# Giving the two chunk halves of a blockwise triangular inverse one signal each and grouping TensorE's matmuls by half

## What is computed

```python
def step(state, inp):
    r_t, w_t, k_t, v_t, a_t, b_t = inp
    sa = jnp.einsum('bhij,bhj->bhi', state, a_t)
    state = (state * w_t[:, :, None, :] + sa[..., None] * b_t[:, :, None, :]
             + v_t[..., None] * k_t[:, :, None, :])
    return state, jnp.einsum('bhij,bhj->bhi', state, r_t)
```

## Time and profile before

| | us |
|---|---|
| median of 3 runs (2155.95 to 2160.34) | 2159.74 |
| the profiled execution | 2153.14 |
| its span | 2151.0 |
| TensorE busy, share of the span | 1959.3, 91% |
| VectorE busy | 988.5, 46% |
| ScalarE busy | 792.0, 37% |

### The profile page before, as it was taken

How to read it: one execution, slowest core, us unless ns; L and a number is a source line. 1 busy time by engine, 2 the same in 40 slices (tenths; PEclk the granted TensorE clock), 3 DMA queues, 4 the chain that set the end, 5 groups by cost and what they waited for, 6 DMA issues and landing times.

```text
span 2151.0 us, 35394 instructions
## 1 busy us (share of the span) xinstructions
PE 1959.3 (91%) x15150; PEld 1549.5 (72%) x15150; DVE 988.5 (46%) x1642; ACT 792.0 (37%) x1323; POOL 142.8 (7%) x126
## 2 busy tenths in 40 slices
PE   3988677777788999999999999999999989999999
PEld 2777365555566788888877777777777777888887
DVE  7443345455544444443335445445445444444422
ACT  4333333333432322222244445445445533222211
POOL 0000323333321000000000000000000000000000
PEclk9999678898998999999999999999999999999999
DMA  2222600000011333333332122222122112333332
GB/s 97 79 78 89 204 2 8 7 8 7 5 64 50 88 96 95 95 101 94 98 89 79 59 69 69 60 69 69 59 69 69 40 59 83 95 96 98 101 97 97
DMA packets 57395, 155.49 MB, mean 72 GB/s; under 512 B 5575, under 2 KB 22135, under 8 KB 57240
## 3 DMA queue, kind: packets, MB, share of 16 engines
q1 hardware_dynamic: 57144, 153.15, 23.5%
q10 hardware_dynamic: 96, 0.07, 0.0%
HBM read 151.03 MB, written 11.61 MB: 76 GB/s over the span
## 4 chain that ended last, share of the span: by engine, by line
PE 86%; DVE 8%; issue 3%; ACT 2%; DMA 1%; POOL 0%; SPq 0%; DVEq 0%; ACTq 0%; POOLq 0%
PE bank L437 83%; PE bank L440 3%; DVE r L1323 1%; DVE f L1409 1%; DVE f L1417 1%; DVE f L1335 1%; DVE f L1392 1%; ACT f L1234 1%; DVE f L1371 0%; DVE f L1422 0%; DVE f L1451 0%; DMA f<-xT 0%; DVE f L1378 0%; DVE f L1465 0%; DVE f L1470 0%
## 5 line engine op out<-in xcount | busy, mean ns | idle before, releaser
L437 PE MATMUL bank<-r 128*128 128x512 f32 x5952 | 1399.9, 396 | 39.5 <-DVE r L1323 22.7
L437 PEld LDWEIGHTS bank<-r 128*128 128x128 f32 x5952 | 1125.2, 190 | 294.1 <-issue 34.6
L437 PE MATMUL bank<-f 64*64 64x64 f32 (+6 forms) x8734 | 525.6, 261 | 143.1 <-DVE f L1302 23.6
L437 PEld LDWEIGHTS bank<-f 64*64 64x64 f32 (+3 forms) x8734 | 375.9, 151 | 281.0 <-issue 147.1
L1291 DVE TENSOR_TENSOR r<-f,r 128x1024 fp32r<-128x1024 f32 x248 | 303.8, 1225 | 502.9 <-ACT r L957 502.6
L957 ACT ACTIVATE r<-f 128x1024 fp32r<-128x1024 f32 x248 | 260.0, 1049 | 157.8 <-PE bank L437 138.2
L1615 DVE TENSOR_TENSOR f<-bank,f 128x512 f32<-128x512 f32 x72 | 55.5, 771 | 134.6 <-PE bank L437 134.3
L1182 ACT ACTIVATE r<-f 128x512 fp32r<-128x512 f32 x44 | 27.8, 632 | 221.9 <-DVE f L1584 221.9
L1208 ACT ACTIVATE f<-bank,f 128x512 f32<-128x512 f32 x48 | 33.0, 687 | 173.5 <-PE bank L437 173.5
L440 PE MATMUL bank<-f 128*128 128x128 f32 x464 | 73.8, 284 | 5.9 <-ACT f L1234 5.5
L1409 DVE TENSOR_TENSOR f<-bank,f 64x512 f32<-64x512 f32 x80 | 55.0, 688 | 50.5 <-PE bank L437 49.2
(11 more groups left out here) (99 smaller groups left out, 965.5 us busy)
## 6 DMA issues: line engine op xcount, KB each, us to landing
f<-stream SPq DMA_DIRECT2D x248, 512.0 KB, 3.6
bias_copies<-bias_rows SPq DMA_DIRECT2D x3, 3072.0 KB, 24.4
f<-xT SPq DMA_DIRECT2D x16, 256.0 KB, 4.3
f<-lora_out SPq DMA_DIRECT2D x16, 128.0 KB, 2.4
f<-bias_copies SPq DMA_DIRECT2D x16, 128.0 KB, 3.3
f<-bias_copies SPq DMA_DIRECT2D x32, 64.0 KB, 3.0
outT<-f SPq DMA_DIRECT2D x8, 256.0 KB, 4.6
f<-const SPq DMA_DIRECT2D x1, 576.0 KB, 4.0
```

Source lines behind the costliest of these rows:

```text
L437: return nc.tensor.matmul(out, lhsT, rhs, start=start, stop=stop, skip_group_check=True)
```

## The change

The two signals `x_ps` and `x_sb`, and `u_ps`, become one signal for each half. `off_diagonal` and `next_inverse` issue all matmuls of half 0 first, then all of half 1, with a wait for each half's own input ahead of its block. VectorE masks half 0 when half 0's products are there and then waits for half 1's. ScalarE's copy waits for half 0 alone, VectorE's for half 1 alone. The matmuls, masks and copies themselves stay the same.

```diff
@@ TensorE, off_diagonal and next_inverse
-                else:
-                    pe.wait_ge(s["u0_sb"], (N_LEV - 1) * hp + n - 1)
-                    pe.wait_ge(s["u1_sb"], (N_LEV - 1) * hp + n - 1)
-                for q in range(NT):
-                    for h in range(2):
-                        for e in range(2):
+                for e in range(2):
+                    if n > 1:
+                        pe.wait_ge(s[f"u{e}_sb"], (N_LEV - 1) * hp + n - 1)
+                    for q in range(NT):
+                        for h in range(2):
                             last = mm(banks[2 + e][CH * e:CH * (e + 1), (h * 4 + q) * CH:(h * 4 + q + 1) * CH],
                                       half(score(O_BU, hp, h, q, 0), 1 - e), half(block64(tu(hp, e), h, q), 1 - e))
-                last.then_inc(s["x_ps"], 1)
+                    last.then_inc(s[f"x_ps{e}"], 1)
...
-                pe.wait_ge(s["x_sb"], 2 * ((N_LEV - 1) * hp + n))
...
-                        if n < N_LEV - 1:
-                            for e in range(2):
-                                mm(to(e, 1 - e), u(e), x(e))
-                        for e in range(2):
-                            last = mm(to(e, e), x(e), u(e))
-                last.then_inc(s["u_ps"], 1)
+                for e in range(2):
+                    pe.wait_ge(s[f"x_sb{e}"], (N_LEV - 1) * hp + n)
+                    for q in range(NT):
+                        for h in range(2):
+                            u, x = half(block64(tu(hp, e), h, q), e), half(block64(O_XI, h, q), e)
+                            to = lambda side: banks[4 + e][CH * side:CH * (side + 1), (h * 4 + q) * CH:(h * 4 + q + 1) * CH]
+                            if n < N_LEV - 1:
+                                mm(to(1 - e), u, x)
+                            last = mm(to(e), x, u)
+                    last.then_inc(s[f"u_ps{e}"], 1)
@@ ScalarE, keep_inverse
-                act.wait_ge(s["u_ps"], (N_LEV - 1) * hp + n)
+                act.wait_ge(s["u_ps0"], (N_LEV - 1) * hp + n)
@@ VectorE, x_masked and keep_inverse
-                dve.wait_ge(s["x_ps"], (N_LEV - 1) * hp + n)
                 for e in range(2):
+                    dve.wait_ge(s[f"x_ps{e}"], (N_LEV - 1) * hp + n)
...
-                       bc(lev, (0, 8), (1, CH)), ALU.mult).then_inc(s["x_sb"], 1)
+                       bc(lev, (0, 8), (1, CH)), ALU.mult).then_inc(s[f"x_sb{e}"], 1)
...
-                dve.wait_ge(s["u_ps"], (N_LEV - 1) * hp + n)
+                dve.wait_ge(s["u_ps1"], (N_LEV - 1) * hp + n)
```

## The result

| | before | changed |
|---|---|---|
| median us | 2160.04 (4 runs, 2155.95 to 2161.38) | 2246.87 (4 runs, 2218.28 to 2279.57) |
| ratio | | 1.0352, 95% interval 1.0271 to 1.0433 |
| profiled execution, its span | 2153.14, 2151.0 | 2218.28, 2216.2 |

What follows compares the result with a forecast made beforehand. The inverses' chain of TensorE steps, masks and copies was taken as the bound on the stretch touched. Iterations of 26.4, 5.6 and 3 us sum to +35 us, giving 2188 or 2195, taken as 2191; range 2168 to 2226.

Steps and rivals of the forecast that it cites:

- The blocks: Both steps of a level: two blocks of 0.93 us overlapping by 0.17 take 1.69 us, 0.76 more than before.
- Level 2: Second inverse level: both steps +0.76 us, gaps -0.10 and -0.44, sum +1.0; period about 5.7 us instead of 4.72.
- Level 4: Fourth inverse level: `off_diagonal`'s surplus hidden behind the path to `a_k_v`, `next_inverse` pays, +0.8 us in a full iteration.
- level 5: Fifth inverse level: +0.76 us, gap to the variance sum -0.52, then +0.76 until `solve`: +1.0 us.
- Level 3: Third inverse level: +0.76 us twice, offset by -0.54 and -0.95 of shorter waits, sum 0 in a full iteration.
- level 1: First inverse level: +1.1 us, or +1.7 where `off_diagonal` runs at the lower clock, in five of six full iterations.
- The sum at equal clock: Whole stretch of the inverses: 26.4 us for six full iterations, +5.6 for the last, +3 for the first, +35 us.
- the rival in which the clock falls in the levels: Inverse levels: ten of 40 wholly at 1.2 GHz add 34 us, giving 2225; twenty give 2259; 9%.
- one in which it rises: Inverse iterations: shorter TensorE waits keep the clock high, 26 us come back, net +9, 2168 us; 10%.
- Full overlap: Both steps: half 1's block starts with half 0's, about 12 us faster, 2148; 5%.
- no overlap: Both steps: blocks run strictly one after another, +0.17 us in about 65 exposed steps, +11, 2202; 11%.
- open weight loads: Both steps: loads not hidden behind matmuls, +1.8 us in each of 65 exposed steps, +117, 2308; 3%.

Runs made afterwards that it cites:

- The pair with added work in the level 4 wait: Changed kernel and kernel before, each with two unread constant matmuls ahead of `a_k_v`: 2206.6 us (ratio 1.0232) and 2157.6 us (1.0007).
- the pair with it in all waits: Changed kernel and kernel before, with unread matmuls ahead of `a_k_v` and in six tail waits: 2177.6 us (ratio 1.0103) and 2139.6 us (0.9941).
- with more quarters filled: Changed kernel with extra unread matmuls in idle array quarters during `off_diagonal` and half 0's block of `next_inverse`: 2214.9 us, ratio 1.0216.
- `off_diagonal` alone: Kernel before with only `off_diagonal` grouped by half, with its own signals and mask waits; `next_inverse` as before: 2176.6 us, ratio 1.0106.
- one bank with added work: Kernel before with `off_diagonal`'s halves in one bank under one mask, plus unread matmuls ahead of `a_k_v` and in tail waits: 2119.9 us, ratio 0.9812.

## Why the prediction was wrong

- **The blocks: right.** A block has a quarter's pace of 58 ns a pass, and the next begins when three are left. Forecast 1.69 us of starts for both blocks of a step; `next_inverse` lasts 1.91 us with its last pass's latency of 0.22.
- **The levels at equal clock: right.** Level 2 +1.0 forecast, and 573.04 - 567.31 = 5.7 us from one copy's end to the next (566.62 + 0.69 to 572.35 + 0.69) against 4.72 is +1.0. Level 4 +0.8 forecast, +0.6 measured; level 5 +1.0 forecast, +1.1 measured. Level 3, which was to stay as it was, takes 5.3 us instead of 5.5. For level 1 no two iterations at equal clock were compared.
- **The sum at equal clock: right.** +35 forecast. The pair with added work in the level 4 wait gives 35.3, the pair with it in all waits 29. The two traced stretches of before and changed differ by 446.5 - 382.6 = 63.9 us, of which 75 us more low time at 0.44 are 33: 31 are left.
- **The clock: wrong, and this is the step that failed.** I priced the low clock only where before had it, in `off_diagonal` of level 1, and otherwise let the sum stand "against the profiled execution's own 2153.1" at its clock of 0.954. I gave 9% to the rival in which the clock falls in the levels, and 10% to one in which it rises. It fell: the median of the five executions has 336 us of low time, against 198 in the profiled execution of before. (336 - 198) x 0.44 = 61 us, with 31 that makes 92, which is what lies between those two executions (2245.2 - 2153.1), and 5 more than the 87 between the medians. The price of 0.44 comes from the changed kernel's own executions, so only the step to the kernel before checks it. The rival's price was too low (3.4 us for a level wholly at 1.2 GHz; level 5 measured 10.5 - 5.7 = 4.8 with its fillers), and I had no reason for its chance. I had read that the short iterations were those with more of the higher clock, and did not ask how the clock came back in them.
- **The waits.** The prediction said that TensorE has shorter waits and took this as speaking for the clock. Shown is that with the level 4 wait filled no low stretch begins in level 4 any more and some 35 us come back, so the wait starts those. Shown also is that steps at least as long with more quarters at work end them after 3.4 us and keep a clock of 0.961. So the wait, which was there before, starts them, and the grouped blocks behind it draw them out. Not shown is how much of the low time each quarter accounts for (with more quarters filled, those that begin in level 4 fell from 92 us to 41), nor whether the number of quarters counts or the number of passes.
- **The rivals.** Full overlap, no overlap and open weight loads are all out by the 1.91 us. On the rule of the Trainium skill ("TensorE: Matmul & The Clock Gate", Part 3, "The mechanism") that weight loads overlap only when the row group differs: grouped blocks stay in one row group and keep 58 ns a pass, so the changed kernel's trace disagrees with it too. The same section of the Trainium skill also has loads pulled ahead when they go to a background weight buffer, which the prediction left out; that clause would fit these traces. On its rule that matmuls keep strict order: in the changed kernel's `off_diagonal` of level 2, where passes otherwise start 58 ns apart, three pairs of them start within 4 to 6 ns of each other at the change of halves, so half 1's block begins while passes of half 0's are still to start, and across two quarters the rule does not hold as it stands.
- **The parts were less even than forecast.** `off_diagonal` alone cost about 5 us at equal clock instead of 17; level 3 gained 0.7 us where it was taken as a loss of 0.2.
- **The signals.** The prediction counted five more waits a level and took them as free. The change adds two waits and two signals a level, and with the order of before they cost 0.07 us in level 2, some 3 us in all.

## What to carry to other kernels

Small matmuls that go to different quarters of the array should stay interleaved; grouping them by chain makes each chain as long as both were, and on an engine whose fillers stand between the steps most of that time is paid. Work in the wait that starts a low stretch was worth some 35 us where the stretch was long, and nothing where it was short. Before a matmul order is changed, look at how the granted clock comes back in the present one, and price the whole stretch at both levels, since the same change cost about 30 us at the clock of before and 87 at the one that it brought. When two engines alternate in a chain, look first at whether the slower step can be done in one instruction instead of two: here that gave 0.9%, and harmless matmuls in the long waits a further 1%.

## What the runs showed of the hardware

- A block of matmuls for one quarter of the array does not end before the next quarter's begins: three passes still start beside it, with 64 columns as with 128.
- The two row halves of the array wrote disjoint partitions of one PSUM bank in the same 1.74 us as two banks.
- At the low clock a grouped level 5 takes 10.5 us against 5.7. Low stretches that begin in level 4 lasted 3.4 us in six of six cases with every matmul doubled in alternating order, 3.4 to 13.7 in the kernel before, and 17.1 to 20.5 in the changed one.
- Two idle matmuls an iteration, 16 in all, took the changed kernel's loss against before from 87 to 52 us and moved the kernel before by nothing; in both traces no low stretch begins in level 4 any more.
- The same program's executions spread over 61 us here, all of it along the granted clock; with the clock near its ceiling (one bank with added work) they spread over 15.
